# Gathering a small expert's tokens: selection stationary in four column tiles, then two transposes

## What is computed

```
combine = sum(one_hot(top_i, 8) * softmax(top_v))       # (256, 8), two entries a row
for e in range(8):
    out += combine[:, e] * ((silu(x @ w_gate[e]) * (x @ w_up[e])) @ w_down[e])
```

## Time and profile before

| what | value |
|---|---|
| median of 3 runs | 1148.76 us (1147.72 to 1149.1) |
| span of the profiled execution | 1147.8 us |
| PE busy | 1113.6 us (97%) |
| DVE, ACT busy | 643.1 us (56%), 466.6 us (41%) |
| expert blocks loaded | 209 of 1 MB, median 8.3 to 8.6 us from issue to landing |
| three gathers (L1983) | from 508.6, 671.6 and 871.5 us |

### The profile page before, as it was taken

The page is one execution under the profiler, slowest core; times in us unless marked ns, Lnnn a source line. Parts: engine busy times, 40 slices in busy tenths (PEclk is TensorE's granted clock), DMA queues, the critical chain, the costliest instruction groups (busy, mean ns, idle before and its releaser), DMA issues.

```text
span 1147.8 us, 14639 instructions
## 1 busy us (share of the span) xinstructions
PE 1113.6 (97%) x5867; PEld 821.7 (72%) x5867; DVE 643.1 (56%) x745; ACT 466.6 (41%) x595; POOL 44.0 (4%) x45
## 2 busy tenths in 40 slices
PE   7999999999999999999999999999999999999996
PEld 6777878888877778776666666666666666666664
DVE  4887675445467876764655534554653465555235
ACT  4656444444335666143344423333342343443220
POOL 3000020000023000000000000000000000000001
PEclk9999999999999999989999999999999999999998
DMA  9943355555547500089999989899999989999962
GB/s 298 339 147 111 104 181 192 183 183 183 183 147 213 218 1 1 1 322 345 358 369 351 342 334 374 294 395 385 337 378 342 374 293 382 372 353 369 360 263 77
DMA packets 126814, 300.08 MB, mean 261 GB/s; under 512 B 4970, under 2 KB 7160, under 8 KB 126736
## 3 DMA queue, kind: packets, MB, share of 16 engines
q1 hardware_dynamic: 124336, 291.52, 70.4%
q0 software_dynamic: 2112, 6.87, 2.2%
q10 hardware_dynamic: 288, 0.63, 0.1%
HBM read 297.88 MB, written 1.12 MB: 260 GB/s over the span
## 4 chain that ended last, share of the span: by engine, by line
PE 89%; DMA 4%; DVE 3%; ACT 2%; issue 2%; POOL 0%; POOLq 0%; SPq 0%; DVEq 0%; ACTq 0%
PE bank L1583 24%; PE bank L1584 22%; PE bank L1645 12%; PE bank L2021 7%; PE bank L1673 6%; PE bank L2031 3%; PE bank L1756 3%; PE bank L1865 2%; DMA raw<-in_w_in 2%; PE bank L1850 1%; PE bank L1782 1%; PE bank L1999 1%; DMA raw<-in_moe_w_down 1%; ACT w_hi L724 1%; PE bank L1983 1%
## 5 line engine op out<-in xcount | busy, mean ns | idle before, releaser
L1423 DVE TENSOR_TENSOR w_lo<-raw,w_hi 128x2048 fp32r<-128x2048 f32 x83 | 190.3, 2292 | 275.7 <-ACT w_hi L905 275.7
L1583 PE MATMUL bank<-w_hi,xT_hi 128*128 128x512 f32 (+1 forms) x832 | 333.3, 402 | 6.1 <-DVE xT_lo L1042 2.1
L1584 PE MATMUL bank<-w_hi,xT_lo 128*128 128x512 f32 (+1 forms) x832 | 323.2, 390 | 0.0
L905 ACT ACTIVATE w_hi<-raw 128x2048 fp32r<-128x2048 f32 x83 | 158.7, 1912 | 246.5 <-PE bank L1645 139.2
L1583 PEld LDWEIGHTS bank<-w_hi,xT_hi 128*128 128x128 f32 x832 | 158.3, 190 | 74.3 <-issue 29.8
L1019 DVE TENSOR_TENSOR w_lo<-raw,w_hi 128x2048 fp32r<-128x2048 f32 x62 | 141.9, 2291 | 104.9 <-ACT w_hi L724 104.5
L1584 PEld LDWEIGHTS bank<-w_hi,xT_lo 128*128 128x128 f32 x832 | 158.4, 190 | 29.4
L1645 PE MATMUL bank<-w_lo,xT_hi 128*128 128x512 f32 (+1 forms) x640 | 167.3, 384 | 0.0
L724 ACT ACTIVATE w_hi<-raw 128x2048 fp32r<-128x2048 f32 x64 | 122.6, 1917 | 99.3 <-PE bank L1645 45.9
L1645 PEld LDWEIGHTS bank<-w_lo,xT_hi 128*128 128x128 f32 x640 | 118.3, 188 | 24.3
L1583 PE MATMUL bank<-w_hi,hT_hi 128*128 128x512 f32 x312 | 124.6, 399 | 2.3 <-issue 2.3
(11 more groups left out here) (206 smaller groups left out, 1027.0 us busy)
## 6 DMA issues: line engine op xcount, KB each, us to landing
raw<-in_moe_w_up SPq DMA_DIRECT2D x70, 1024.0 KB, 8.6
raw<-in_moe_w_down SPq DMA_DIRECT2D x70, 1024.0 KB, 8.3
raw<-in_moe_w_gate SPq DMA_DIRECT2D x69, 1024.0 KB, 8.3
raw<-in_w_in SPq DMA_DIRECT2D x23, 1024.0 KB, 9.2
raw<-in_ffn_w_gate SPq DMA_DIRECT2D x11, 1024.0 KB, 5.2
raw<-in_ffn_w_up SPq DMA_DIRECT2D x11, 1024.0 KB, 5.1
raw<-in_ffn_w_down SPq DMA_DIRECT2D x11, 1024.0 KB, 5.0
raw<-in_w_out SPq DMA_DIRECT2D x8, 1024.0 KB, 6.1
```

The costliest lines, as they stand in the source:

```text
L905: nc.scalar.activation(w_hi[:, m % NH, :], raw[:, n % NR, :], ACT.Copy).then_inc(hi_done, 1)
L1423: nc.vector.tensor_tensor(w_lo[:, m % NH, :], raw[:, (BASE_MOE + load[at[o]]) % NR, :], w_hi[:, m % NH, :].bitcast(F32), ALU.subtract).the ...
L1583: nc.tensor.matmul(o, hi, wh, start=start, stop=False)
L1584: nc.tensor.matmul(o, lo, wh, start=False, stop=False)
```

## The change

The gather becomes two steps. `gather_rows` makes the selected tokens as rows: `sel` (128x32) is stationary, `xtok` moves, 256 features in each of four column tiles, for two token tiles, so eight float32 matmuls; column tile g holds features 256g to 256g+255 of the 32 slots, and they fill columns 0 to 255 of bank 5. ACT copies them to a new buffer `xg` (`gathered_rows`). One unit later `gather` transposes the two 128x128 halves of `xg` to columns 256 to 511 of bank 5, and ACT copies those to `xs` with the features put in order. `gathers_behind` now gives the unit of the rows; the transposes and the `xs` copy come behind the unit that follows. For the first small expert of TRIO the rows stand behind unit 0 and the transposes behind unit 1. In REST both stand before unit 0. On ACT the `xs` copy now stands ahead of the unit's weight split. Two semaphores are new, and `bank5_read` waits for the copy of the rows too.

```diff
-            first = {-1 if units is REST else 1: 0}
+            first = {-1 if units is REST else 0: 0}
...
+            def gathered_rows(item):
+
+                act.wait_ge(rows_psum, item + 1)
+                nc.scalar.activation(xg[:], bank[:, 5, 0:D // 4], ACT.Copy).then_inc(rows_in, 1)
+
             def gathered(item):
 
                 act.wait_ge(gather_psum, item + 1)
-                nc.scalar.activation(xs[:], bank[:, 5, 0:KT * SMALL].rearrange("p (k j) -> p k j", j=SMALL),
+                nc.scalar.activation(xs[:].rearrange("p (g a) j -> p a g j", a=2),
+                                     bank[:, 5, D // 4:D // 2].rearrange("p (a g j) -> p a g j", a=2, j=SMALL),
                                      ACT.Copy).then_inc(g_in, 1)
...
+                    if u and u - 1 in gathers:
+                        gathered(fix(small + gathers[u - 1]))
                     if u in at[0:-AHEAD]:
                         large_split(at, load, at.index(u) + AHEAD, off, use)
...
                     if u in gathers:
-                        gathered(fix(small + gathers[u]))
+                        gathered_rows(fix(small + gathers[u]))
...
+            def gather_rows(item):
+
+                pe.wait_ge(sel_ready, item + 1)
+                for tt in range(NT):
+                    for g in range(4):
+                        ins = nc.tensor.matmul(bank[g * SMALL:(g + 1) * SMALL, 5, 0:D // 4], sel[:, tt, 0:SMALL],
+                                               xtok[:, tt, g * (D // 4):(g + 1) * (D // 4)], start=(tt == 0), stop=(tt == NT - 1))
+                ins.then_inc(rows_psum, 1)
+
             def gather(item):
 
-                pe.wait_ge(sel_ready, item + 1)
-                for kt in range(KT):
-                    for tt in range(NT):
-                        ins = nc.tensor.matmul(bank[:, 5, kt * SMALL:(kt + 1) * SMALL], xtok[:, tt, kt * P:(kt + 1) * P],
-                                               sel[:, tt, 0:SMALL], start=(tt == 0), stop=(tt == NT - 1))
+                pe.wait_ge(rows_in, item + 1)
+                for a in range(2):
+                    ins = nc.tensor.transpose(bank[:, 5, D // 4 + a * P:D // 4 + (a + 1) * P], xg[:, a * P:(a + 1) * P], ident)
                 ins.then_inc(gather_psum, 1)
...
+                rows_behind(-1)
                 gather_behind(-1)
...
-                    gather_behind(u)
+                    rows_behind(u)
+                    if u:
+                        gather_behind(u - 1)
```

More of the change, by code:

```diff
@@ L262, in encoder @@
             xs = sb("xs", [P, KT, SMALL], scope=s)
+            xg = sb("xg", [P, D // 4], scope=s)
             hs = sb("hs", [P, NF, SMALL], scope=s)
@@ L381, in encoder @@
         s_in = sem("s_in")
+        rows_psum = sem("rows_psum")
+        rows_in = sem("rows_in")
         gather_psum = sem("gather_psum")
@@ L960, in run_units @@
                 if -1 in gathers:
+                    gathered_rows(fix(small + gathers[-1]))
                     gathered(fix(small + gathers[-1]))
@@ L2046, in run_units @@
                 ahead = large_before(units)
-                made = {"small": 0, "sel": 0, "gather": 0, "adds": 0}
+                made = {"small": 0, "sel": 0, "rows": 0, "gather": 0, "adds": 0}
                 spots = [(spot, k, quarters) for k in range(3) if ("S", k, "gate", 0, 0) in units
@@ L2056, in bank5_read @@
                         pe.wait_ge(selT_in, fix(small + made["sel"]))
+                    if made["rows"]:
+                        pe.wait_ge(rows_in, fix(small + made["rows"]))
                     if made["gather"]:
@@ L2059, in bank5_read, with rows_behind @@
                     pe.wait_ge(added, done + made["adds"])
+                def rows_behind(u):
+                    if u in gathers:
+                        bank5_read()
+                        gather_rows(fix(small + gathers[u]))
+                        made["rows"] += 1
                 def gather_behind(u):
```

## The result

The changed kernel takes 1137.31 us (median of 5 runs, 1136.98 to 1139.2) and the kernel before 1149.1 us beside it (5 runs, 1147.72 to 1151.69): the ratio is 0.99, 95% interval 0.9883 to 0.9916. The profiled execution of after took 1139.2 us, with a span of 1137.3 us and a mean granted clock of 0.993; before's span was 1147.8, its clock 0.991. So the two spans are 10.5 us apart, and that is what their rows have to explain.

A forecast was written before the change was run, and what follows sets the result against it. TensorE was taken to bound the kernel; gathers bring 3.55 + 2.78 + 2.78, together 9.1 us, cut by late blocks to 3.3 + 2.5 + 2.4 = 8.2: 1148.76 - 8.2 = 1140.6 us, range 1138.5 to 1144.0.

The forecast's parts named there:

- What bounds the kernel, and that the gain is kept: Expert stage: TensorE, busy 97% of the span, bounds; what leaves it comes off the time unless what comes next is late.
- Rows: Row products at each gather take 0.87 us; with mode changes between two L units, 1.30 us.
- B: At each gather, row products go at the weight loads' pace, 1.85 us: 6.2 us gained, 1142.6; chance 0.14.
- E: At each gather, the four column tiles run one after another, 3.5 us: 1.2 us gained, 1147.6; chance 0.06.
- F: At each gather, tiles run in turn with weight loads not hidden, 5.3 us: 4.2 us slower, 1153; chance 0.04.
- Transposes, copies, selection: Two transposes cost 0.29 us at gather 1, 0.17 at 2 and 3; copies are covered, nothing waits for the selection.
- The sum on TensorE: Gather 1 brings 3.55 us, gathers 2 and 3 2.78 each, together 9.1 us before late blocks.
- The clock term: Lower clock behind old gather 1 costs 1.40 us, which the change removes; gathers 2 and 3 have none.
- Rival C: The lower clock stays behind gather 1, which then brings 2.15 us: sum 7.1, time 1141.7; chance 0.08.
- What is late next: Blocks landing behind the gathers cut their gains to 3.3, 2.5 and 2.4 us, 8.2 in all.
- Rival D: The transfers keep gather 1's gain, every block coming when it came: 4.9 us left, 1143.9; chance 0.06.
- The range: Whole kernel: 1138.5 (9.1 us gained with no late block, 0.7 us run spread below) to 1144.0 us.

The follow-up runs named there:

- experiment 8: The changed kernel with its eight row products issued twice, the second time over the same result: 1142.7 us, ratio 0.9942.
- experiment 9: The changed kernel with both transposes directly behind the rows, no unit between: 1144.98 us, ratio 0.9964.
- before_again: The kernel before, run again with no edit: 1150.07 us, ratio 1.001.
- g1_new: The changed kernel with gathers 2 and 3 put back to the old form, only gather 1 new: 1147.05 us, ratio 0.9989.
- experiment 4: The changed kernel with gather 1 put back to the old form, gathers 2 and 3 new: 1140.59 us, ratio 0.9933.
- experiment 3: The changed kernel with only gather 1 in the new form, gathers 2 and 3 old: 1147.05 us, ratio 0.9989.
- experiment 6: The kernel before with all old gathers in pieces, gather 1 in two halves, 2 and 3 in four pieces each: 1145.9 us, ratio 0.9975.
- split_old: The kernel before with old gather 1 in two halves, behind units 0 and 1: 1147.32 us, ratio 0.9985.
- after_again: The changed kernel, run again with no edit: 1139.13 us, ratio 0.9916.
- split_all: The kernel before with all three old gathers issued in pieces, same instructions: 1145.9 us, ratio 0.9975.
- old_twice: The kernel before with each old gather issued twice, the second time over the first: 1169.81 us, ratio 1.0185.
- no_cover: The changed kernel with the transposes directly behind the rows, so no unit covers the rows' copy: 1144.98 us, ratio 0.9964.

## Why the prediction was right or wrong

**What bounds the kernel, and that the gain is kept: right.** TensorE's chain had 89% and now has 88%; of the 3.66 + 2.8 + 2.8 = 9.3 us less on it in this pair, all but 0.6 us came off the time.

**Rows: right.** 0.87 by experiment 8, and 1.25 between two L units (forecast 1.30). Rivals B, E and F fall with it: the eight products of 256 columns in four tiles take what one further S unit takes, not the time of the load pace or of tiles in turn.

**Transposes, copies, selection: right.** 0.27 at gather 1 (0.29); 866.85 - 866.68 = 0.17 at gather 3 (0.17); the copy ended 0.3 us before it was due in gather 2, just as worked out; experiment 9 shows that without its cover it would cost 3.3 and 0.7 us and more.

**The sum on TensorE for this pair of profiles: right.** 3.66, 2.80, 2.80 against 3.55, 2.78, 2.78.

**The clock term: the step that failed.** "Behind these two the L unit runs at its usual pace, so they have no clock term" read a property of the place out of one execution. It was right for that execution and wrong for the kernel: the lower level follows an unbroken old gather in 5 of 11 cases, and at each of the three places in some (1 of 3, 1 of 4 and 3 of 4). The term was sized at 1.40 us, for one gather always; what it measured is about 3 us in all, near 1 us for each gather. The windows of before_again and g1_new show the misplacement, and with them experiment 4 (gathers 2 and 3 worth 7.7 us, 5.4 to 10.0, not 4.9) and experiment 3 (gather 1 worth 1.3, at most 2.9, not 3.3); the size comes from the clocks of the runs and from experiment 6, which are rougher. Of the distance between the 8.2 forecast and the mean gain of 10.2 us, this term has about 1.6 (3 - 1.4) and the late blocks 0.3 (0.9 - 0.6). Rival C, the clock staying low behind the new gather 1, is not borne out: the clock is full behind the new gather 1 in all five profiles that have it with its cover, and behind all 15 new gathers, although two transposes stand there; the rule of the Trainium skill (TensorE: Matmul & The Clock Gate, Part 4) that transposes do not count as busy isn't contradicted by it, as 0.27 us of them is little, but it has no weight here.

**What is late next: failed in its sizes.** The forecast cut 0.25 + 0.28 + 0.38, 0.9 us in all (the last by its own rows 0.3, as 890.29 - 887.8 leaves 2.5 us and not 2.4); measured was 0.6 + 0 + 0. At gathers 2 and 3 it took a block as late from the moment its weight load was due. After's own rows show why that is too strict; its S pair behind gather 2, weight loads and matmuls:

```profile
675.45 0.16 PEld L2050 LDWEIGHTS bank<-raw,hs 128*32 128x32 f32 x8 [0.35 <-issue]
675.45 1.92 PE L2050 MATMUL bank<-raw,hs 128*32 128x512 f32 x16
676.28 0.18 PEld L2050 LDWEIGHTS bank<-raw,hs 128*32 128x32 f32 x8 [0.68 <-DMA raw<-in_moe_w_down]
677.30 0.19 PEld L1595 LDWEIGHTS bank<-w_hi,xT_hi 128*128 128x128 f32 x1 [0.84 <-issue]
```

The second load waits 0.68 us for its block where 0.30 is usual, and the pair still takes 677.30 - 675.45 = 1.85 us, against 1.86 undisturbed: the matmuls of the first unit run on over the wait. About 0.4 us of lateness is free. At gather 1 the same allowance holds, but the shift was larger than the forecast's by the 0.65 us that after was ahead, so the load was due at 527.60 - 4.29 = 523.31 and came at 524.29: 0.98 us late, of which 0.6 remained. Rival D (the transfers keep gather 1's gain) is out: they kept a sixth.

**The range: too narrow below.** Its low end was put at 1138.5, where its own working, 1148.76 - 9.1 - 0.7, gives 1139.0. It took the spread of the runs from three runs that lay 1.4 us apart. Before's 61 runs have a standard deviation of 2.2 us and go from 1144.5 to 1155.9. With a clock term of up to three times 1.4 in place of 1.4, and the same 0.7 for the spread, the low end would have been about 1136 (1139.0 - 2.8). The measured 1137.31 also lies in the lower half of the changed kernel's runs (17 runs, median 1138.2), so 0.9 us of the miss of 1.2 is the draw of the first set.

**Open.** The 1.45 us near the end of the stage in the first pair of profiles. There, the same 21 units take 59.90 us in before and 60.12 in before_again, 59.36 in g1_new and 59.33 in split_old, but 58.36 in after, 58.48 in after_again, and between 57.9 and 58.5 in all the other profiles. It hangs on when one block lands: before waits 1.14 us for it, after doesn't. It doesn't follow the form of the gathers alone, since split_all (58.32) and old_twice (58.02) have old gathers only. But all six profiles with gathers 2 and 3 new are short, and all four long ones have these two gathers old and unbroken. So some of the gain that is put down to the clock above, up to 1.5 us, may come from this block, which the forecast didn't look at. Against it stands that the clocks of the runs leave 6.5 to 7.1 us for everything else, and the gathers' rows fill that. No run was made to part the two. Open too is the difference between the clock's part by counting (2.5) and by the runs' clocks (3.1 to 3.7); 11 old gathers are few.

## What to carry to other kernels

A stretch in which TensorE is busy with narrow matmuls (here 32 columns behind each 128x128 weight load, 3.7 us of them) was followed by the lower clock in 5 of 11 cases here, in some executions and not in others: ask this at each place where such a stretch stands, from several executions, and put its mean cost into the sum and its whole spread into the range. Put other work of TensorE between a product and the transposes that need its copy, and look at what the copying engine has queued ahead. An operand that landed 0.4 us after its weight load was due cost nothing here, while the matmuls before it still ran.

## What the runs showed of the hardware

- In one profile the lower clock follows a stand: behind TensorE's 3.29 us wait in no_cover the granted clock of the next 4 us is 0.59, in a place where after has 1.00.
- Doubling the narrow stretch more than doubles its price: 11.1 us of further matmuls cost 21.2 us. In and behind the third doubled gather the granted clock was 0.50 in three windows of 4 us in a row, 13.7 us in all, while TensorE was busy in every one of them for the whole 4.00 us.
- The spread of this kernel's times, 11 us between the extremes of 61 runs, goes mostly with the clock: around a line of 1.0 us for each 0.001 of mean granted clock their standard deviation is 1.2 us, where it is 2.2 without.
- In four column tiles at work the time goes by the columns through each tile: a second set of row products (eight fp32 products of 256 columns) costs 0.87 us, as does one more S unit (four of 512).
